# A two-block transformer forward: the opening projection by channel halves, and the modulation sums in another order

## The chip, the cores and the metric

One NeuronCore of a Trainium2 chip runs the whole program. The metric is the device time of one execution in microseconds (us); lower is better. Engines are named as the profile names them: PE is TensorE (PEld its weight loads), DVE is VectorE, ACT is ScalarE, POOL is GpSimd, SP is SyncE, which here only issues DMA transfers.

## What is computed

The reference is two blocks over 256 tokens of 1024 channels, all in float32. Only the head of block one matters for the change; in the reference it reads

```python
for l in range(DEPTH):
    mod = c @ w_ada[l] + b_ada[l]
    shift, scl, gate = jnp.split(mod, 3, axis=-1)
    h = rms_norm(x, g_norm[l]) * (1.0 + scl[:, None, :]) + shift[:, None, :]
    proj = h @ w_in[l]
    u_pool, z_pool, q, k, v, z_attn, m_pool, m_attn = jnp.split(proj, splits, axis=-1)
```

`mod` is a matrix times a vector (1024 by 3072); `h` is the normalised input, scaled and shifted per channel; `proj` is a 256x1024 by 1024x5120 product. After it come a pooling branch and an 8-head attention branch, two up-projections and an output projection. Block two has a modulation of its own (`w_ada_2`, 1024 by 6144), another input projection, retention and sparse attention, and a last layer that reads every row of two 16384x1024 tables.

## The kernel before, in words

**Panels.** Every weight matrix is cut into panels of 128 partitions by 4096 floats (2.1 MB): all 1024 input channels (8 groups of 128) for 512 output columns. The list `STREAM` names the panels in the order in which they are loaded, with their user: `"pe"` for a product on PE, `"dve"` for a modulation sum, `"row"` for a modulation panel that PE multiplies itself. Four slots in SBUF hold them; panel n goes into slot n mod 4. SP issues two transfers for each panel, one for each half (four channel groups), after it has waited until panel n-4 is used up (`panel_used`). `ada1` are the panels of `w_ada` (0, 1 shift, 2, 3 scale, 4, 5 gate; the even one for channels 0 to 511), `in1` those of `w_in`, `ada2` those of `w_ada_2`, `out1` the output projection.

**Modulation sums.** For a `"dve"` panel DVE forms the sum of the eight channel groups, each times a column of `c` (`ada`, `sum_step`: one tensor_scalar and seven scalar_tensor_tensor of 128x512). The running sum lies in SBUF (`acc`) for the first three, in a PSUM bank for those of block one after them, and in SBUF again for the last ones. Then PE adds up the partitions with a product by ones (step `("ada", n)`, or `start_columns` in the opening), and DVE adds the bias and stores scale or shift (`ada_out`, `start_scale`). `next_acc` at the end of a `proj` step says how far ahead of its panel a sum is made: all those whose panel stands less than 3 places behind the projection's panel, except the last two of the list (`ada_steps[:-2]`).

**Products in three thirds.** A float32 product is made as three faster ones, of a high part and a low part of each operand. ACT copies a half panel to its high part (`unit_high`, L814, step `("high", k)`), POOL subtracts to get the low part (`unit_low`, L740, four instructions for each half panel), and `products` (L1123, L1129, L1135) issues 24 matmuls of 128x512 for each half panel: high by high, low input by high weight, high input by low weight. `UNITS` lists the half panels in the order in which both are made. The input `h` itself is made from transposes (`xT`, L1068): ACT writes the modulated channels of token tile 1 and DVE those of tile 0 (L852, L1735), ACT makes their high part (L799), DVE the low part (L1807).

**Order.** `steps()` writes one list, and every engine walks it and does its own part of each step. Inside `heads`, the list mixes the eight attention heads (`score`, `pT`, `pv`) with the projections that follow. PSUM banks 0 to 3 are handed out in turn to the steps that need one, and a step waits until the use before it is freed.

**The opening.** SP loads ada1 2, 3, 0, 1 and then in1 2 and 3. DVE sums panels 2, 3 and 1; PE multiplies panel 0 as a row (`make_row`), ACT copies the row, and PE turns it into columns (`row_columns`). After all four, `mod_ready` goes up once, and ACT and DVE write `h` for all eight channel groups; then PE starts the product of in1 2. The rest of the modulation alternates with the panels of `in1` (ada1 4, in1 4, ada1 5, in1 5, ...).

## Time and profile before

| | us |
|---|---|
| runs, median of 3 | 1271.54 |
| lowest and highest run | 1267.73, 1272.63 |
| profiled execution, its own time | 1268.93 |
| its span in the trace | 1267.1 |
| PE busy in the span | 1193.6 |
| DVE, ACT, POOL busy | 904.5, 619.4, 551.6 |

The page gives one profiled execution: busy time of each engine, the span in 40 slices, the groups of instructions that cost most, and for the idle time before a group what ended it. A timeline row has start, duration, engine, line, operation, what is written from what, the count that was merged into the row, and in brackets the idle time before it with its releaser. A granted clock of 1.00 is 2.4 GHz on PE, 0.50 is 1.2 GHz. Times in the trace count from the start of the span.

### The profile page before, as it was taken

To read this page: it belongs to the slowest core of one execution; us is meant where nothing else is said; L and a number is where in the kernel's file an instruction comes from. 1 tells how busy PE (TensorE), PEld (TensorE's weight loads), DVE (VectorE), ACT (ScalarE), POOL (GpSimd) and SP (SyncE) were. 2 spreads that over 40 slices of the span, in tenths; PEclk is the share of its full clock that TensorE was granted. 3 is DMA by queue.
4 is the path that set the end of the run, shared out by engine and by line. 5 is a ranking of instruction groups with operands and counts; after the bars stand their busy time and mean duration, and the time that the engine had idled before them with its cause. 6 is when DMAs were issued, how large, how long until landed. Compare 5 with 4: busy or idle time off the path is not lost.

```text
span 1267.1 us, 19098 instructions
## 1 busy us (share of the span) xinstructions
PE 1193.6 (94%) x7186; PEld 1050.7 (83%) x7186; DVE 904.5 (71%) x1847; ACT 619.4 (49%) x1077; POOL 551.6 (44%) x323
## 2 busy tenths in 40 slices
PE   4899998899968899999999999999999999999996
PEld 2778876686747699999999999999888888888885
DVE  5678657676685643999948999999566656656566
ACT  2454444444533434444456666555445545444543
POOL 0968759474531202888877777766300000000000
PEclk9899999999978999999999999999999999999998
DMA  9988664354231431565544545455566666666664
GB/s 374 417 329 323 265 266 169 133 206 154 113 150 67 199 133 49 182 184 182 185 160 160 161 156 165 152 153 152 164 231 206 209 231 218 197 185 196 190 196 149
DMA packets 54523, 244.28 MB, mean 193 GB/s; under 512 B 6944, under 2 KB 7328, under 8 KB 42016
## 3 DMA queue, kind: packets, MB, share of 16 engines
q1 hardware_dynamic: 54000, 242.34, 55.4%
q8 instruction: 58, 0.95, 0.3%
q10 hardware_dynamic: 432, 0.72, 0.2%
q14 instruction: 33, 0.27, 0.1%
HBM read 240.94 MB, written 2.10 MB: 192 GB/s over the span
## 4 chain that ended last, share of the span: by engine, by line
PE 75%; DVE 4%; issue 1%; ACT 1%; POOL 0%; POOLq 0%; DVEq 0%; ACTq 0%
PE bank L1526 10%; PE bank L1523 10%; PE bank L1522 10%; PE banks L1562 5%; PE bank L1565 5%; PE bank L1568 5%; PE banks L1565 5%; PE bank L1562 5%; PE banks L1568 5%; PE banks L1536 3%; PE banks L1123 1%; PE banks L1129 1%; PE banks L1135 1%; PE banks L1393 1%; PE banks L1481 1%
## 5 line engine op out<-in xcount | busy, mean ns | idle before, releaser
L765 POOL TENSOR_TENSOR split_r<-ring,split_r 128x1024 fp32r<-128x1024 f32 x128 | 308.0, 2407 | 158.0 <-ACT split_r L996 157.9
L996 ACT ACTIVATE split_r<-ring 128x1024 fp32r<-128x1024 f32 x256 | 269.1, 1052 | 180.2 <-PE bank L1526 180.2
L1522 PE MATMUL bank<-h_high_r,split_r 128*128 128x256 f32 x1024 | 251.3, 283 | 1.7 <-ACT split_r L996 1.7
L1523 PE MATMUL bank<-h_low_r,split_r 128*128 128x256 f32 x1024 | 251.2, 283 | 0.0
L2147 DVE TENSOR_TENSOR split_r<-ring,split_r 128x1024 fp32r<-128x1024 f32 x128 | 156.8, 1225 | 65.6 <-ACT split_r L996 65.6
L1522 PEld LDWEIGHTS bank<-h_high_r,split_r 128*128 128x128 f32 x1024 | 196.3, 192 | 1.9 <-issue 1.9
L1523 PEld LDWEIGHTS bank<-h_low_r,split_r 128*128 128x128 f32 x1024 | 196.4, 192 | 0.0
L740 POOL TENSOR_TENSOR wq_low_r<-G,G_r 128x512 fp32r<-128x512 f32 (+1 forms) x104 | 135.2, 1336 | 68.5 <-ACT G_r L814 68.5
L769 POOL TENSOR_TENSOR small<-small 128x1 f32<-128x1 f32 x2 | 1.5, 760 | 359.0 <-DVE small L2173 359.0
L1526 PE MATMUL bank<-h_high_r,split_r 128*128 128x256 f32 x1024 | 143.7, 283 | 0.2 <-POOL split_r L765 0.2
L1050 ACT ACTIVATE gs_r<-G 128x256 fp32r<-128x256 f32 x128 | 53.5, 418 | 172.5 <-PE bank L1568 172.5
L1526 PEld LDWEIGHTS bank<-h_high_r,split_r 128*128 128x128 f32 x1024 | 132.1, 192 | 0.4 <-POOL split_r L765 0.4
L2095 DVE SCALAR_TENSOR_TENSOR hot_r<-bank,x,w_both_r 128x256 fp32r<-128x256 f32 x256 | 105.5, 473 | 0.0
L2145 DVE TENSOR_TENSOR gs_r<-G,gs_r 128x256 fp32r<-128x256 f32 x128 | 54.3, 424 | 61.8 <-ACT gs_r L1050 61.4
L740 POOL TENSOR_TENSOR wq_low_r<-G,hT_r 128x512 fp32r<-128x512 f32 x48 | 65.3, 1394 | 66.0 <-ACT hT_r L814 66.0
L1562 PE MATMUL banks<-split_r,gs_r 128*128 128x512 f32 x254 | 79.1, 393 | 1.8 <-ACT split_r L996 1.8
L1565 PE MATMUL bank<-split_r,gs_r 128*128 128x512 f32 x254 | 78.2, 389 | 0.0
L1562 PE MATMUL bank<-split_r,gs_r 128*128 128x512 f32 x254 | 78.2, 389 | 0.0
L1568 PE MATMUL banks<-split_r,gs_r 128*128 128x512 f32 x254 | 78.2, 389 | 0.0
L1568 PE MATMUL bank<-split_r,gs_r 128*128 128x512 f32 x254 | 78.2, 389 | 0.0
L1565 PE MATMUL banks<-split_r,gs_r 128*128 128x512 f32 x254 | 78.2, 389 | 0.0
L814 ACT ACTIVATE G_r<-G 128x2048 fp32r<-128x2048 f32 (+1 forms) x26 | 48.7, 1881 | 21.9 <-DMA G<-in_in 18.8
(453 smaller groups left out, 2242.1 us busy)
## 6 DMA issues: line engine op xcount, KB each, us to landing
ring<-in_down SPq DMA_DIRECT2D x128, 512.0 KB, 3.5
ring<-in_up SPq DMA_DIRECT2D x128, 512.0 KB, 3.5
G<-in_ada SPq DMA_DIRECT2D x32, 1024.0 KB, 10.5
G<-in_in SPq DMA_DIRECT2D x32, 1024.0 KB, 7.0
G<-in_out SPq DMA_DIRECT2D x8, 1024.0 KB, 8.1
G<-in_wq SPq DMA_DIRECT2D x8, 1024.0 KB, 7.7
tab<-in_ada SPq DMA_DIRECT2D x4, 1024.0 KB, 5.8
G<-in_poolup SPq DMA_DIRECT2D x2, 1024.0 KB, 6.1
```

Source lines behind the costliest of these rows:

```text
L740: pool.tensor_tensor(low[:, c, :], raw_half[:, c, :], high[:, c, :].bitcast(F32), ALU.subtract)\
L765: pool.tensor_tensor(wsplit[:, j % SPLIT, 1, :], raw[:, j % RAW, :], wsplit[:, j % SPLIT, 0, :].bitcast(F32), ALU.subtract).then_inc(low_r ...
L996: nc.scalar.activation(wsplit[:, n % SPLIT, 0, :], raw[:, n % RAW, :], ACT.Copy).then_inc(high_ready, 1)
L1522: mm(o, w[0][:, c, :], h_high[:, c, :], start=(c == 0), stop=False)
L1523: mm(o, w[0][:, c, :], h_low[:, c, :], start=False, stop=False)
L1526: ins = mm(o, w[1][:, c, :], h_high[:, c, :], start=False, stop=(c == C - 1))
L1562: mm(o, g[0][:, tok], w[:, 0, cols], start=(n == 0), stop=False, skip_group_check=True)
L1565: mm(o, g[1][:, tok], w[:, 0, cols], start=False, stop=False, skip_group_check=True)
L1568: ins = mm(o, g[0][:, tok], w[:, 1, cols], start=False, stop=False, skip_group_check=True)
L2095: ins = stt(out=O2[m % 2][:, t, :, :], in0=iota_p.unsqueeze(1).to_broadcast([P, 2, P]), scalar=picks[:, 1, tok:tok + 1], in1=w_both[:, :, ...
L2145: tt(gs[n % 2][1], Gv[:, n, :], gs[n % 2][0].bitcast(F32), ALU.subtract).then_inc(gs_low, 1)
L2147: tt(wsplit[:, n % SPLIT, 1, :], raw[:, n % RAW, :], wsplit[:, n % SPLIT, 0, :].bitcast(F32), ALU.subtract)\
```

## The change

**Order of the loads.** `STREAM` now begins ada1 2, 0, 3, in1 2, in1 3, ada1 1, and afterwards each pair has the `in1` panel first and the modulation panel second. The loads are issued from a list `LOADS`: the first halves of in1 2 and in1 3 are loaded ahead of ada1 1, their second halves behind it. Three rows of gate constants (1.5 MB) are loaded behind in1 5 and no longer behind in1 2, with a semaphore of their own.

**Opening by halves.** DVE sums ada1 2 and ada1 0, which are scale and shift of channels 0 to 511, and `mod_ready` goes up for these alone. `h` is made for them, and PE multiplies the first half of in1 2. PE makes the row from ada1 3 in two parts, with `start_columns(1)` between them. The step `mods` sums ada1 1 on DVE with the running sum in PSUM bank 7, and PE's `row_columns` and `start_columns(2)` stand between the first half of in1 2 and that of in1 3. The second halves of both follow. ACT makes the high parts of three half panels (`("high", 1)` to `("high", 3)`) ahead of the second part of `h`.

**Sums in the rest of block one.** The sum for a projection is now that of the panel just behind it, and `ada_steps[:-4]` leaves the last four to be placed by hand. The sum of ada2 6 (panel 22) is written into the list as single steps: four behind `upT` and four behind the first half of `poolup`, in SBUF. Its product by ones, and that of ada2 9, stand behind the last head.

PE in the opening: the names are `keep,tab` for columns from a sum (4 matmuls), `keep,G` 128x128 for the transposes, `G,small` for the row, `keep,G` 128x1 for its columns; then the thirds of a half panel, 8 matmuls each. Before:

```order
L1099 MATMUL banks<-keep,tab 128x1 x4
L1068 MATMUL bank<-keep,G 128x128 x8
L1068 MATMUL banks<-keep,G 128x128 x8
L1099 MATMUL banks<-keep,tab 128x1 x4
L1085 MATMUL bank<-G,small 1x512 x8
L1092 MATMUL bank<-keep,G 128x1 x4
L1099 MATMUL bank<-keep,tab 128x1 x4
L1123 MATMUL bank<-hT_0_r,ring_r 128x512 x8
L1129 MATMUL bank<-hT_0_r,G_r 128x512 x8
L1135 MATMUL bank<-wq_low_r,ring_r 128x512 x8
```

and with the change:

```order
L1105 MATMUL banks<-keep,tab 128x1 x4
L1075 MATMUL bank<-keep,G 128x128 x8
L1075 MATMUL banks<-keep,G 128x128 x8
L1090 MATMUL bank<-G,small 1x512 x4
L1105 MATMUL banks<-keep,tab 128x1 x4
L1090 MATMUL bank<-G,small 1x512 x4
L1129 MATMUL banks<-hT_0_r,ring_r 128x512 x8
L1135 MATMUL banks<-hT_0_r,G_r 128x512 x8
L1141 MATMUL banks<-wq_low_r,ring_r 128x512 x8
L1098 MATMUL bank<-keep,G 128x1 x4
L1105 MATMUL bank<-keep,tab 128x1 x4
L1129 MATMUL bank<-G_r,ring_r 128x512 x8
```

The row's columns and the third set of columns have moved behind the first half panel's 24 matmuls; the next half panel stands behind them.

DVE behind the last head: `tab<-G,small` is a sum (`tab<-G,small,tab` its steps in SBUF), `G_r<-...,ring_r` the low part of the pooled rows, `G<-G,bank` the evacuation of a half of `poolup`, `G<-bank,G` the step `y`. Before:

```order
L1978 TENSOR_TENSOR G_r<-banks,ring_r 128x4x128 x2
L1934 SCALAR_TENSOR_TENSOR G<-G,bank 128x512
L1934 SCALAR_TENSOR_TENSOR G<-G,banks 128x512
L1918 TENSOR_TENSOR G<-bank,G 128x512 x2
L1663 TENSOR_SCALAR tab<-G,small 128x512
L1665 SCALAR_TENSOR_TENSOR tab<-G,small,tab 128x512 x3
L1692 TENSOR_TENSOR small<-bank,small 128x4
```

and with the change:

```order
L2007 TENSOR_TENSOR G_r<-banks,ring_r 128x4x128
L2007 TENSOR_TENSOR G_r<-bank,ring_r 128x4x128
L1682 TENSOR_SCALAR tab<-G,small 128x512
L1684 SCALAR_TENSOR_TENSOR tab<-G,small,tab 128x512 x3
L1963 SCALAR_TENSOR_TENSOR G<-G,banks 128x512 x2
L1684 SCALAR_TENSOR_TENSOR tab<-G,small,tab 128x512 x4
L1947 TENSOR_TENSOR G<-bank,G 128x512 x2
L1682 TENSOR_SCALAR tab<-G,small 128x512
L1684 SCALAR_TENSOR_TENSOR tab<-G,small,tab 128x512 x3
L1716 TENSOR_TENSOR small<-bank,small 128x4
L1719 TENSOR_SCALAR small<-small 128x4
L1720 TENSOR_TENSOR small<-small 128x4
```

Eight sum steps have come in, four on either side of the evacuations, ahead of `y`; so has one more set of columns (three small instructions).

The diff, cut to what the prediction speaks of:

```diff
 STREAM = []
-STREAM += [("ada1", 2, PANEL, "dve"), ("ada1", 3, PANEL, "dve"), ("ada1", 0, PANEL, "row"), ("ada1", 1, PANEL, "dve")]
-STREAM += [("in1", 2, PANEL, "pe"), ("in1", 3, PANEL, "pe")]
-for a, b in ((("ada1", 4), ("in1", 4)), (("ada1", 5), ("in1", 5)), (("ada2", 2), ("in1", 0)), (("ada2", 3), ("in1", 1)),
-             (("ada2", 0), ("in1", 6)), (("ada2", 1), ("in1", 7)), (("ada2", 8), ("in1", 8)), (("ada2", 9), ("in1", 9))):
-    STREAM += [(*a, PANEL, "dve"), (*b, PANEL, "pe")]
+STREAM += [("ada1", 2, PANEL, "dve"), ("ada1", 0, PANEL, "dve"), ("ada1", 3, PANEL, "row"), ("in1", 2, PANEL, "pe"),
+           ("in1", 3, PANEL, "pe"), ("ada1", 1, PANEL, "dve")]
+for a, b in ((("in1", 4), ("ada1", 4)), (("in1", 5), ("ada1", 5)), (("in1", 0), ("ada2", 2)), (("in1", 1), ("ada2", 3)),
+             (("in1", 6), ("ada2", 0)), (("in1", 7), ("ada2", 1)), (("in1", 8), ("ada2", 8)), (("in1", 9), ("ada2", 9))):
+    STREAM += [(*a, PANEL, "pe"), (*b, PANEL, "dve")]
...
 START = 3
+LOADS = [(0, 0), (0, 1), (1, 0), (1, 1), (2, 0), (2, 1), (3, 0), (4, 0), (5, 0), (5, 1), (3, 1), (4, 1)]
+LOADS += [(n, half) for n in range(6, len(STREAM)) for half in range(2)]
...
 UNITS = [(AT[p], half) for p in SPLIT_PANELS for half in range(2)]
+UNITS[1:3] = UNITS[2:0:-1]
...
-    ada_after(AT[("in1", 2)], ada)
-    high("in1", 2, (0,))
-    out.extend(("xT", 0, t, half) for t in range(NT) for half in range(2))
-    high("in1", 2, (1,))
-    panel("in1", 2)
+    ada_after(AT[("in1", 4)], ada)
+    out.extend([("high", 0), ("xT", 0, 0, 0), ("xT", 0, 1, 0), ("xsplit", 0), ("row",), ("high", 1), ("high", 2), ("high", 3),
+                ("mods",), ("xT", 0, 0, 1), ("xT", 0, 1, 1), ("xsplit", 1), ("proj", "in1", 2, 0), ("proj", "in1", 2, 1)])
     panel("in1", 3)
     panel("in1", 4)
...
-    later += [[("upT", 0), ("upT", 1), ("high", 21)],
-              [("high", 22), ("up", "poolup", 0, 0), ("up", "poolup", 1, 0)]]
+    six = AT["ada2", 6]
+    later += [[("upT", 0), ("upT", 1), ("high", 21)] + [("sum", six, c) for c in range(4)],
+              [("high", 22), ("up", "poolup", 0, 0), ("up", "poolup", 1, 0)] + [("sum", six, c) for c in range(4, C)]]
     heads(0, H, later)
...
+            bank = 4 + s[2]
         else:
             bank = turn % 4
...
-            for n, (name, i, cols, user) in enumerate(STREAM):
-                if n >= SLOTS:
+            for n, half in LOADS:
+                name, i, cols, _ = STREAM[n]
+                if n >= SLOTS and half == 0:
...
-                if n == SLOTS:
+                if (n, half) == (4, 1):
                     sp.dma_start(tab[:, 0:n_tab], d["tab"]).then_inc(tables_in, 16)
-                    sp.dma_start(gateA, d["gate1"].partition_broadcast(P)).then_inc(tables_in, 16)
-                    sp.dma_start(gateB, d["gate3"].partition_broadcast(P)).then_inc(tables_in, 16)
-                    sp.dma_start(gfin, d["gfin1"].partition_broadcast(P)).then_inc(tables_in, 16)
-                if n == 2 * SLOTS:
+                if (n, half) == (2 * SLOTS, 1):
+                    sp.dma_start(gateA, d["gate1"].partition_broadcast(P)).then_inc(gates_in, 16)
+                    sp.dma_start(gateB, d["gate3"].partition_broadcast(P)).then_inc(gates_in, 16)
+                    sp.dma_start(gfin, d["gfin1"].partition_broadcast(P)).then_inc(gates_in, 16)
+                if (n, half) == (2 * SLOTS + 2, 1):
                     sp.dma_start(band, d["band"]).then_inc(band_in, 16)
                     sp.dma_start(wgrp, d["wgrp"]).then_inc(band_in, 16)
...
-            act.wait_ge(row_full, 1)
-            nc.scalar.activation(row, ps[6][0:1, :], ACT.Copy).then_inc(row_copied, 1)
...
+                elif kind == "row":
+                    act.wait_ge(row_full, 1)
+                    nc.scalar.activation(row, ps[6][0:1, :], ACT.Copy).then_inc(row_copied, 1)
+                elif kind == "xsplit":
+                    for q in range(NT):
+                        x0_high_part(q, s[1])
...
-                    if half == 0:
-                        act.wait_ge(mod_ready, blk_n + 1)
+                    act.wait_ge(mod_ready, half + 1)
...
-                    for q in range(NT):
-                        x0_high_part(q, half)
...
+            def make_row(half):
+
+                w = wait_panel(pe_, ROWS[0], (half,)).rearrange("p (c n) -> p c n", c=C)
+                for c in range(4 * half, 4 * half + 4):
+                    ins = mm(ps[6][0:1, :], c1[:, c:c + 1], w[:, c, :], start=(c == 0), stop=(c == C - 1))
+                if half == 1:
+                    ins.then_inc(row_full, 1)
...
-                    ins = mm(ps[4 + k][:, c:c + 1], acc[k % 2][:, c * P:(c + 1) * P], ones[:, 0:1], start=True, stop=True)
+                    ins = mm(ps[(2, 3, 6)[k]][:, 4 * (k == 2) + c:4 * (k == 2) + c + 1], acc[k % 2][:, c * P:(c + 1) * P], ones[:, 0:1], start=True, stop=True)
...
+            for half in range(2):
+                for t in range(NT):
                     pe_.wait_ge(xn_ready, t + 1)
-                transposes(("xT", 0, t, half), [xn[0][:, t, (4 * half + c) * P:(4 * half + c + 1) * P] for c in range(4)])
+                    transposes(("xT", 0, t, half), [xn[0][:, t, (4 * half + c) * P:(4 * half + c + 1) * P] for c in range(4)])
+            make_row(0)
             start_columns(1)
-            make_row()
-            row_columns()
-            start_columns(2)
+            make_row(1)
+
...
+            def in1_products(i, halves, fill):
...
+            in1_products(2, (0,), True)
+            row_columns()
+            start_columns(2)
+            in1_products(3, (0,), True)
+            in1_products(2, (1,), False)
+            in1_products(3, (1,), False)
...
-                part = ps[4 + k % 2][:, :] if START <= k < BLOCK_ONE else a
+                part = ps[7][:, :] if k == START - 1 else ps[4 + k % 2][:, :] if START <= k < BLOCK_ONE else a
...
-            def start_scale(k):
-
-                dve.wait_ge(start_cols, k + 1)
-                c4 = slice(4 * k, 4 * k + 4)
-                link(tt(modA[:, 0, c4], ps[4 + k][:, 0:4], b1c[:, 8 + 4 * k:12 + 4 * k], ALU.add))
+            def start_scale(half, src):
+
+                c4 = slice(4 * half, 4 * half + 4)
+                link(tt(modA[:, 0, c4], src[:, 0:4], b1c[:, 8 + 4 * half:12 + 4 * half], ALU.add))
                 link(ts(modA[:, 0, c4], modA[:, 0, c4], 1.0, None, ALU.add))
                 link(tt(modA[:, 0, c4], modA[:, 0, c4], gcol[:, 0, c4], ALU.mult))
+
+            def start_shift(half, src):
+
+                c4 = slice(4 * half, 4 * half + 4)
+                link(tt(modB[:, 0, c4], src[:, 0:4], b1c[:, c4], ALU.add))
+                dve.sem_inc(mod_ready, 1)
 
             dve.wait_ge(first_in, 16)
             next_acc()
             next_acc()
             dve.wait_ge(consts_in, 16 * 7)
-            for k in range(2):
-                start_scale(k)
-            next_acc()
-            dve.wait_ge(row_cols, 1)
-            tt(modB[:, 0, 0:4], ps[7][:, 0:4], b1c[:, 0:4], ALU.add)
-            dve.wait_ge(start_cols, 3)
-            link(tt(modB[:, 0, 4:8], ps[6][:, 0:4], b1c[:, 4:8], ALU.add))
-            dve.sem_inc(mod_ready, 1)
+            dve.wait_ge(start_cols, 1)
+            start_scale(0, ps[2])
+            dve.wait_ge(start_cols, 2)
+            start_shift(0, ps[3])
...
-                elif s == ("xT", 0, 1, 1):
...
+                elif kind == "mods":
+                    next_acc()
+                    dve.wait_ge(row_cols, 1)
+                    dve.wait_ge(start_cols, 3)
+                    start_scale(1, ps[6])
+                    start_shift(1, ps[6][:, 4:8])
+                elif kind == "xsplit":
+                    half = s[1]
+                    dve.wait_ge(x0_high_ready, 2 + 2 * half)
+                    for t in range(NT):
+                        evacuated(dve, ("xT", 0, t, half))
...
-                    ahead = [a for a in ada_steps[:-2] if a[1] < AT[(s[1], s[2])] + 3]
+                    ahead = [a for a in ada_steps[:-4] if a[1] < AT[(s[1], s[2])] + 3]
```

## Rows read from the trace of the kernel before

**Rows 1.** Stretches of PE alone: us, busy, PE clock, DMA share, GB/s.

```profile
20.40:22.40 2.00, 0.89 (x8) 1.00 1.01 422
...
35.60:38.80 3.20, 3.10 (x7) 0.50 1.05 416
...
43.60:49.10 5.50, 5.50 (x25) 1.00 1.01 422
...
72.00:188.00 116.00, 113.25 (x582) 1.00 0.73 292
```

**Rows 2.** Timeline of DVE in the opening: start, us, instruction, idle before.

```profile
15.46 0.49 DVE L1663 TENSOR_SCALAR tab<-G,small 128x512 f32<-128x512 f32 x1 [2.49 <-DMA G<-in_ada]
15.98 5.48 DVE L1665 SCALAR_TENSOR_TENSOR tab<-G,small,tab 128x512 f32<-128x512 f32 x7
...
25.51 0.48 DVE L1663 TENSOR_SCALAR tab<-G,small 128x512 f32<-128x512 f32 x1 [2.27 <-DMA G<-in_ada]
...
35.54 1.62 DVE L1807 TENSOR_TENSOR G_r<-G,ring_r 128x1024 fp32r<-128x1024 f32 x1
```

**Rows 3.** Timeline of PE in the opening.

```profile
22.49 7.03 PE L1085 MATMUL bank<-G,small 128*1 128x512 f32 x16
...
31.56 1.05 PE L1099 MATMUL bank<-keep,tab 128*128 128x1 f32 x8 [0.31 <-DVE tab L1665]
...
35.70 3.75 PE L1123 MATMUL bank<-hT_r,ring_r 128*128 128x512 f32 x8 [3.09 <-DVE G L1735]
...
60.85 2.08 PE L1123 MATMUL bank<-G_r,ring_r 128*128 128x512 f32 x8 [0.48 <-issue]
```

**Rows 4.** Timeline of ACT in the opening.

```profile
30.37 1.91 ACT L814 ACTIVATE hT_r<-G 128x2048 fp32r<-128x2048 f32 x1
...
32.97 1.50 ACT L852 ACTIVATE G<-banks,small 128x128 f32<-128x128 f32 x4 [0.68 <-DVEq L1777]
34.36 1.15 ACT L799 ACTIVATE ring_r<-G 128x512 fp32r<-128x512 f32 x2
```

**Rows 5.** Timeline of POOL, opening and last heads.

```profile
32.36 5.95 POOL L740 TENSOR_TENSOR wq_low_r<-G,hT_r 128x512 fp32r<-128x512 f32 x4 [17.10 <-ACT hT_r L814]
...
185.99 5.23 POOL L740 TENSOR_TENSOR wq_low_r<-G,G_r 128x512 fp32r<-128x512 f32 x4
191.19 6.34 POOL L740 TENSOR_TENSOR wq_low_r<-G,ring_r 128x512 fp32r<-128x512 f32 x4
198.64 6.92 POOL L740 TENSOR_TENSOR wq_low_r<-G,hT_r 128x512 fp32r<-128x512 f32 x4 [1.11 <-ACT hT_r L814]
```

**Rows 6.** Line 1665 until 215 us: ns min/median/max, first and last start.

```profile
L1665 DVE SCALAR_TENSOR_TENSOR banks<-G,small,banks x54: 754/756/757, 52.5 to 168.7; 128x512 f32<-128x512 f32 x54
L1665 DVE SCALAR_TENSOR_TENSOR tab<-G,small,tab x28: 739/752/1670, 7.5 to 201.0; 128x512 f32<-128x512 f32 x28
```

**Rows 7.** Timeline of DVE behind the last head.

```profile
184.45 0.69 DVE L1934 SCALAR_TENSOR_TENSOR G<-G,bank 128x512 f32<-128x512 f32 x1 [4.33 <-PE bank L1135]
185.36 0.69 DVE L1934 SCALAR_TENSOR_TENSOR G<-G,banks 128x512 f32<-128x512 f32 x1 [0.22 <-PE banks L1135]
187.22 1.29 DVE L1918 TENSOR_TENSOR G<-bank,G 128x512 f32<-128x512 f32 x2 [1.17 <-PE bank L1310]
188.72 1.35 DVE L1663 TENSOR_SCALAR tab<-G,small 128x512 f32<-128x512 f32 x1 [0.22 <-DVE G L1918]
190.11 5.04 DVE L1665 SCALAR_TENSOR_TENSOR tab<-G,small,tab 128x512 f32<-128x512 f32 x3
195.18 0.16 DVE L1692 TENSOR_TENSOR small<-bank,small 128x4 f32<-128x4 f32 x1
```

**Rows 8.** Timeline of PE behind the last head.

```profile
186.95 1.00 PE L1197 MATMUL bank<-keep,tab 128*128 128x1 f32 x8
...
195.49 0.63 PE L1068 MATMUL bank<-keep,G 128*128 128x128 f32 x4 [1.51 <-DVE small L1692]
```

**Rows 9.** Timeline of ACT: the first high part of poolup.

```profile
166.86 1.92 ACT L814 ACTIVATE ring_r<-G 128x2048 fp32r<-128x2048 f32 x1 [2.47 <-DMA G<-in_poolup]
```

More of the change, by code:

```diff
@@ L246 @@
             bank = 4 + s[3]
+        elif s[0:2] == ("xT", 0) and s[3] == 1:
+            bank = 4 + s[2]
         else:
@@ L835, in _ @@
                     if (t, half) == (0, 0):
-                        act.wait_ge(mod_ready, b + 1)
+                        act.wait_ge(mod_ready, b + 2)
                     dst, ready = (x1_high, x1_high_ready) if b == 1 else (h_high, h_high_ready)
@@ L1091, in row_columns @@
                 for c in range(4):
-                    ins = mm(ps[7][:, c:c + 1], row[:, c * P:(c + 1) * P], ones[0:1, 0:1], start=True, stop=True)
+                    ins = mm(ps[6][:, c:c + 1], row[:, c * P:(c + 1) * P], ones[0:1, 0:1], start=True, stop=True)
                 ins.then_inc(row_cols, 1)
@@ L1206, in _ @@
                     if t == 0:
[L1207 to L1214 removed]
+                        in1_products(i, (0, 1), True)
                 elif kind in ("unit", "third"):
@@ L1683, in ada_out @@
                     g = gateA if name == "ada1" else gate2
+                    if name == "ada1" and half == 0:
+                        dve.wait_ge(gates_in, 48)
                     if name == "ada2" and half == 0:
```

54 lines of the change are left out of this document (22 added, 32 removed).

## Prediction

> **What bounds the kernel now.** I read the stretches of the trace first, then the timelines of all engines in the opening and behind the last head. From 72 to 188 us PE is busy 113.25 of 116 us at full clock [rows 1]: time won before 72 us is carried on, and time lost behind 188 us is not given back by it. Only two places are left in which the change can act: the opening, where PE waits for the modulation, and the place behind the last head, to which the sum of ada2 6 has been moved.
>
> In the opening the loads are the bound. The core takes 420 GB/s [rows 1], which is 2.5 us for each half panel (1.05 MB); the first half of ada1 3 has landed when DVE starts on it at 15.46, that of ada1 1 four half panels later, at 25.51 [rows 2]. PE starts its first product only at 35.70, after a wait of 3.09 us [rows 3]: the modulation of all channels comes ahead of it (ada1 1 landed, summed by 31.5, columns at 31.56). That product runs at a granted clock of 0.50, half of 2.4 GHz [rows 1], so that 8 matmuls take 3.75 us; at 43.6 the clock is 1.00 and 25 matmuls take 5.50. A half panel of 24 matmuls is thus 5.45 us, including its weight waits. In1 4 starts at 60.85 [rows 3].
>
> **The opening, step by step.** The loads in the new order land, at 2.5 us each from the anchor 15.5: ada1 0 at 15.5 and 18.0, ada1 3 at 20.5 and 23.0, the first halves of in1 2 and in1 3 at 25.5 and 28.0, ada1 1 at 30.5 and 33.1, the second halves at 35.6 and 38.1, the tables at 41.2, in1 4 at 43.7 and 46.2.
> - DVE ends its second sum at 21.5 as before (15.98 plus 5.48 [rows 2]). PE's first row half takes half of 7.03 us [rows 3], from 20.5 to 24.0, and the columns 1.05: shift and scale of the first channels are there at 25.4. That costs nothing, because ACT makes the high part of in1 2 first: 25.5 to 27.5 [rows 4].
> - ACT then writes `h` (1.50) and its high parts (1.15) [rows 4]: 30.2. PE's first product starts there, 5.5 us earlier than 35.70. DVE's low part takes 1.6 [rows 2]; POOL's low weights, 5.95 from 27.5 [rows 5], come at 33.5 and are needed at 33.9. The half panel ends at 35.7.
> - DVE's sum of ada1 1 starts at 31.8, behind that low part. In PSUM a step is 0.76 us as in SBUF [rows 6], 6.2 us for eight: 38.0. PE waits for it from 36.2, and with it the first half of in1 3, which is queued behind; columns until 39.1. That half ends at 44.6.
> - Columns to scale and shift (0.7, with POOL busy perhaps 2.5), `h` and high parts (2.7) end at 44.5 at the latest, so the second halves follow without a wait: in1 2 ends at 50.0, in1 3 at 55.5. POOL's four units of 5.0 to 5.2 us end at 48.7 and are no bound. Their high parts lie in ACT's waits; were they late, POOL's last unit (needed at 53.6) would have 5 us to spare.
> - In1 4 (landed at 46.2) starts at 55.6 instead of 60.85: **5.2 us won**. This needs full clock. The idle stretches are 1.7 us (28.5 to 30.2) and 2.0; 1.1 us idle at 20.4 to 22.4 left the clock at 1.00, 3.09 us brought it to 0.50 [rows 1, 3]. The new ones lie between. One stretch of 3 us at half clock costs 1.5; I take off half of that, 0.8. **Term: -4.4**, bounds -5.2 and -2 (the full loss as in [rows 3], 3.2 us).
>
> Costed at nothing: the later modulation panels. Each is now issued behind its in1 panel and summed one projection later, but the sum (6.3 us) still fits in a projection of 11; one set of columns (1.00 us on PE [rows 8]) only moves to the end. The gate constants now load behind in1 5, 15 us before its use. A second cost hides there: ada2 6 stands ahead of poolup in SP's queue and waits for in1 8, so poolup, whose high part starts at 166.86 upon its landing [rows 9], lands 5 us later. ACT's evacuations of in1 9 stand behind it, 1.7 us late at most, against a set of columns that has gone (-0.9): I take +0.
>
> **Behind the last head.** I count in the times of before; the shift of the opening comes on top. The sum of ada2 6 used to be made during in1 9, with its partial in PSUM. Now its eight steps are in SBUF: four behind the low part of the pooled rows, where DVE was idle for 4.33 us, and four behind the evacuation that ends at 186.05 [rows 7]. POOL works there without a pause until 197.5 [rows 5]. A step in SBUF beside a busy POOL is 1.67 us (three in 5.04 [rows 7]; the longest of 28 is 1.670, of the 54 in PSUM 0.757 [rows 6]). So the first four fit roughly; the second four end at 186.05 + 6.7 = 192.8.
> - PE wants this sum's columns behind those of ada2 9, at 187.9 (186.95 plus the one more set [rows 8]), and the second half of poolup is queued behind: PE stands for 4.9 us.
> - On DVE `y`, at 187.22 before [rows 7], starts at 192.8; the four steps of ada2 7 behind it (1.35 and 5.04) and the new set of columns (0.5) put the one that frees PE's bank from 195.18 to about 201. PE waited for just this (1.51 us at 195.49 [rows 8]), then ACT turns out the heads and makes the high part with which POOL starts at 198.64 [rows 5]; POOL is then busy for 30 us. So the delay is passed on.
> - Delay 5.9, less some tenths because POOL may be through before DVE's last steps. **Term: +5.5.** Lower bound: steps at the 0.78 us spacing of the opening (5.48 for seven [rows 2]), 3.1 us for four, delay 1.9. Upper bound: 8, if the first four run over as well.
>
> Nearest to the truth is the row at 190.11: the same operation, with POOL in the same work, 4 us further on. The Trainium skill, SBUF — State Buffer, section Who interferes with whom, is harsher: a DVE instruction with two SBUF inputs and a POOL instruction that reads SBUF lock each other out for whole instructions. By that rule a step behind one of POOL's 1.25 us instructions would be 2.0 us, four would be 8.1, and the term would be +7 to +8; the longest step in the trace, 1.67, is less than that.
>
> **Sum.** -4.4 + 5.5 = +1.1. The profiled execution had 1268.93 us, so its successor would have 1270.0; the median of the runs, 1271.54, lies 2.6 above it, and with +1.1 becomes **1272.6 us**. A difference of under 0.5% (6.4 us) is about what a measurement of this kernel can't tell from none, so I forecast no change.
>
> **Rivals.**
> - *The sum stops PE and the stop costs the clock* (slower). PE idle for 5 us at 188 to 193 is longer than the 3.09 that brought 0.50 in the opening, and the second half of poolup would then run at half rate (16 matmuls at 0.43 instead of 0.23, +3.2) while POOL is late too: delay 9.5. It decides if the opening also loses its 3.2: -2 + 9.5 = +7.5, **1279.0**. Against it: DVE's chain covers PE's half rate in part. Chance 0.15.
> - *The sums find gaps and the opening runs at full clock* (faster). Delay 1.9; the opening wins the 5.5 of its start and all of the lost 3.2, if the sum of ada1 1 is early enough for PE not to stand: -8.7 + 1.9 = -6.8, **1264.7**. For it: 4 of the 8 steps lie in a stretch where DVE was idle. Against it: POOL is busy from 181 to 197.5, and the sum of ada1 1 can't start before 31.8. Chance 0.12.
> - *The change does not do what it says*: the first product starts early, but PE soon waits for ada1 1 and for the low weights, and in1 4 starts where it did. 0 + 5.5 = +5.5, **1277.0**, still within 0.5%. Chance 0.12.
>
> The forecast itself has 0.61. Faster by over 0.5% is 0.12, slower 0.15, and 0.61 + 0.12 = 0.73 within it. The range runs from the forecast's bounds, -5.2 + 1.9 = -3.3 and -2 + 8 = +6, with 1.5 to 2.5 us for the spread of the runs on either side: 1265.5 to 1279.0. It leaves out the second rival and half of the first, about 0.2.
>
> **What would show it.** Right: first product at about 30, in1 4 at 55 to 57; DVE's SBUF steps of ada2 6 at 1.67 us beside POOL; a wait of PE of some 5 us for `acc` ahead of the second half of poolup; POOL's unit behind 198.64 only 0 to 2 us from where it was. Wrong: no such wait, or steps of 0.75 there (then the loss is mis-sized and the kernel is faster by 3 or more); or a start of in1 4 at 59 or later (then the opening's gain is).

## The result, and the profile after

| | before | after |
|---|---|---|
| median of 20 runs, us | 1269.65 | 1273.26 |
| lowest, highest | 1266.64, 1272.82 | 1270.68, 1286.21 |
| profiled execution: own time, span | 1268.93, 1267.1 | 1271.72, 1269.9 |
| mean granted clock | 0.980 | 0.975 |
| PE, DVE, ACT, POOL busy | 1193.6, 904.5, 619.4, 551.6 | 1199.7, 916.3, 619.4, 554.7 |

The ratio is 1.0039, with a 95% interval of 1.0025 to 1.0053. The quotient of the two medians is 1.0028, and their difference +3.6 us; the forecast was +1.1 and no change by more than 0.5%. The interval lies above 1, so the change is a little slower. Four of the change's 20 runs lie at 1278 to 1286 us; the highest of before is 1272.82. Where ratios and medians disagree below, both are given.

First the opening. Timeline of PE after:

```profile
29.52 2.08 PE L1129 MATMUL banks<-hT_r,ring_r 128*128 128x512 f32 x8 [1.02 <-ACT ring_r L803]
...
36.89 1.05 PE L1105 MATMUL bank<-keep,tab 128*128 128x1 f32 x8 [0.68 <-DVE tab L1684]
37.80 3.67 PE L1129 MATMUL bank<-G_r,ring_r 128*128 128x512 f32 x8
...
57.09 2.08 PE L1129 MATMUL banks<-G_r,ring_r 128*128 128x512 f32 x8 [1.10 <-issue]
```

The first product starts at 29.52 and no longer at 35.70 [rows 3]. PE waits 0.68 us for the sum of ada1 1, then 8 matmuls take 3.67 us (2.08 at 29.52), which is the half clock again. In1 4 starts at 57.09 in place of 60.85: 3.8 us won. Its wait of 1.10 us ("issue") is explained by DVE, which frees the bank only now:

```profile
53.93 1.35 DVE L1661 TENSOR_TENSOR G<-G,ring 128x64 f32<-128x64 f32 x1
55.20 1.32 DVE L1662 TENSOR_TENSOR G<-G,ring 128x64 f32<-128x64 f32 x1
56.44 0.55 DVE L1846 COPY G<-banks 128x384 f32<-128x384 f32 x1
```

The copy ends at 56.99 and PE starts 0.1 us later. The two instructions ahead of it, on 128x64, take 1.35 and 1.32 us beside POOL; in the opening alone (below), where POOL had nothing to do at that point, the same two took 0.23 and 0.22. With one set of columns moved away, the lead at the first head is 4.57 us (75.57 before, 71.00 after), and PE carries it to the last heads.

Then the last head. PE after:

```profile
174.72 0.90 PE L1308 MATMUL bank<-keep,ring 128*128 128x128 f32 x3 [2.64 <-DVE ring L1745]
...
176.55 3.76 PE L1129 MATMUL banks<-ring_r 128*128 128x512 f32 x8
...
191.01 1.84 PE L1223 MATMUL banks<-keep,tab 128*128 128x1 f32 x8 [3.92 <-DVE tab L1684]
192.71 2.05 PE L1129 MATMUL banks<-hT_r,ring_r 128*128 128x512 f32 x4
...
202.75 1.17 PE L1129 MATMUL banks<-G_r,ring_r 128*128 128x512 f32 x4 [0.83 <-ACT ring_r L937]
```

and the same two places of PE before:

```profile
177.83 0.55 PE L1289 MATMUL bank<-keep,ring 128*128 128x128 f32 x3 [1.18 <-DVE ring L1724]
...
179.62 1.16 PE L1123 MATMUL bank<-ring_r 128*128 128x512 f32 x4 [0.63 <-DVE G_r L1978]
...
187.81 1.17 PE L1123 MATMUL bank<-hT_r,ring_r 128*128 128x512 f32 x4
...
196.90 1.16 PE L1123 MATMUL bank<-G_r,ring_r 128*128 128x512 f32 x4 [0.78 <-ACT ring_r L930]
```

DVE and POOL after, over the same stretch:

```profile
169.43 0.90 DVE L1719 TENSOR_SCALAR small<-small 128x4 f32<-128x4 f32 x1
170.37 1.18 DVE L1720 TENSOR_TENSOR small<-small 128x4 f32<-128x4 f32 x1
...
172.82 1.18 DVE L1734 TENSOR_SCALAR small<-small 128x2 f32<-128x2 f32 x1
...
177.44 4.14 DVE L1684 SCALAR_TENSOR_TENSOR tab<-G,small,tab 128x512 f32<-128x512 f32 x3
...
185.10 5.77 DVE L1684 SCALAR_TENSOR_TENSOR tab<-G,small,tab 128x512 f32<-128x512 f32 x4
```

```profile
169.04 4.95 POOL L746 TENSOR_TENSOR wq_low_r<-G,ring_r 128x512 fp32r<-128x512 f32 x4 [12.61 <-ACT ring_r L818]
...
177.87 6.09 POOL L746 TENSOR_TENSOR wq_low_r<-G,hT_r 128x512 fp32r<-128x512 f32 x4 [3.89 <-ACT hT_r L818]
...
204.49 6.74 POOL L746 TENSOR_TENSOR wq_low_r<-G,hT_r 128x512 fp32r<-128x512 f32 x4 [8.16 <-ACT hT_r L818]
```

Two of the small instructions of DVE before:

```profile
174.21 0.16 DVE L1699 TENSOR_TENSOR small<-small 128x4 f32<-128x4 f32 x1
...
176.96 0.17 DVE L1713 TENSOR_SCALAR small<-small 128x2 f32<-128x2 f32 x1
```

Windows of PE after, at the two stretches behind its waits (us, busy, granted clock, DMA share, GB/s):

```profile
176.00:180.00 4.00, 4.00 (x12) 0.50 0.99 420
...
192.00:196.00 4.00, 4.00 (x12) 0.50 0.93 346
```

Read together they give a ledger of after minus before, at the start of the same work of PE:

| place | before | after | difference | step |
|---|---|---|---|---|
| first head | 75.57 | 71.00 | -4.57 | |
| last head's transposes | 177.83 | 174.72 | -3.11 | +1.46 |
| evacuation of poolup's first half ends (DVE) | 186.05 | 185.18 | -0.87 | +2.24 |
| second half of poolup | 187.81 | 192.71 | +4.90 | +5.77 |
| attnup | 196.90 | 202.75 | +5.85 | +0.95 |
| low third behind POOL's unit | 242.62 | 248.29 | +5.67 | -0.18 |
| transposes of block two | 276.78 | 280.54 | +3.76 | -1.91 |
| end | 1267.1 | 1269.9 | +2.8 | -0.96 |

The four plus steps are these. (1) Poolup lands when it did (its high part is made at 167.05, before at 166.86) though all else is 4.6 us earlier, so POOL's unit for it, 169.04 to 173.99, lies over DVE's small instructions of the last head: three take 0.90 to 1.18 us, each of which took 0.16 or 0.17 us before. (2) Behind the wait of 2.64 us the clock is 0.50. (3) PE stands for 3.92 us in front of the sum of ada2 6, and its columns, the additional set, take 1.84 us at half clock and not 1.00: 5.76 of the 5.77. (4) The second half of poolup starts at half clock too. When PE comes to the transposes behind it, at 200.89, it doesn't wait: DVE had freed their banks by 198.46. So in the change it is PE's own row that brings the delay to attnup.

### The profile page after: what moved, and what is told of

Same layout as the page of the kernel before. It is cut to its first block, busy times and chain, and to the rows that moved or that the text cites. A ratio compares the mean times of both kernels' runs of the same rounds, so it can differ in the third digit from the quotient of the medians.

```text
span 1269.9 us, 19103 instructions
## 1 busy us (share of the span) xinstructions
PE 1199.7 (94%) x7186; PEld 1054.6 (83%) x7186; DVE 916.3 (72%) x1847; ACT 619.4 (49%) x1077; POOL 554.7 (44%) x323
## 4 chain that ended last, share of the span: by engine, by line
PE 74%; DVE 4%; issue 1%; ACT 1%; POOL 0%; POOLq 0%; DVEq 0%; ACTq 0%
PE bank L1545 10%; PE bank L1542 10%; PE bank L1541 10%; PE banks L1581 5%; PE bank L1581 5%; PE banks L1587 5%; PE bank L1584 5%; PE bank L1587 5%; PE banks L1584 5%; PE banks L1555 3%; PE banks L1129 1%; PE banks L1135 1%; PE banks L1141 1%; PE bank L1412 1%; PE banks L1160 1%; PE banks L1169 1%
```

## The experiments

Each kernel was timed in 8 to 12 runs beside runs of before on the same chip; the second time is the median of these. Kernels that start from the change have "change" over their diff.

**The change again.** No edit.

> The change once more, as it is, for a second profile and for a ratio on the chip of the next runs. Theory A (what the change loses it loses in three places, each time in the same way): 3 to 4 us above before, with PE idle for 2.6 us near 172 us, idle for 3.9 us near 187 us, and both stretches behind them at a granted clock of 0.50. Theory B (the clock falls by chance): the same time on average, but the granted clock stays at 1.00 behind one of the two waits.

1273.11 us against 1269.69 before, ratio 1.0028 (1.0016 to 1.0040). In its profile PE waits 2.71 us at 174.51 and 4.00 us at 190.72, and the granted clock is 0.50 in 176 to 180 and in 188 to 196. Theory A: the two falls come back.

**Poolup loaded first.** Change:

```diff
-STREAM += [("ada2", 6, PANEL, "dve"), ("poolup", None, PANEL, "pe"), ("attnup", None, PANEL, "pe"), ("ada2", 7, PANEL, "dve"),
+STREAM += [("poolup", None, PANEL, "pe"), ("ada2", 6, PANEL, "dve"), ("attnup", None, PANEL, "pe"), ("ada2", 7, PANEL, "dve"),
...
-    for n in ada_after(AT[("poolup", None)], ada):
+    for n in ada_after(AT[("attnup", None)], ada):
```

> Poolup is loaded ahead of ada2 6; all else as in the change. Theory A (poolup lands late, so that POOL's unit for it, 169.0 to 174.0, lies over DVE's small instructions of the last head, three of which take 0.9 to 1.2 us in place of 0.17; PE then waits 2.6 us and loses its clock): the unit starts near 164, the small instructions take 0.17 us, PE waits 1.2 us at the last head, the granted clock is 1.00 behind it, and the end comes 3 to 4 us earlier, about the time of before. Theory B (DVE's sums behind the last head set the time, whatever comes ahead of them): no gain, the time of the change within 1 us. Theory C (ada2 6, now landing 5 us later, is late for its sum at 177): the wait of PE at 187 grows by up to 4 us, and nothing is won.

1273.71 against 1269.69, ratio 1.0030 (1.0015 to 1.0046): nothing won. PE:

```profile
173.12 0.55 PE L1308 MATMUL bank<-keep,ring 128*128 128x128 f32 x3 [1.18 <-DVE ring L1745]
...
174.91 3.54 PE L1129 MATMUL banks<-ring_r 128*128 128x512 f32 x8 [0.64 <-DVE G_r L2007]
```

The step from load to small instructions is right: POOL's unit is at 164.26, the scalar instruction takes 0.17 us, the wait is 1.18 us. Three things work against the gain. The clock fell all the same (3.54 us for 8 matmuls); the wait for ada2 6 was 4.49 us, where that of the change repeated was 4.00; and out1 0, whose slot is now that of poolup, landed only at 204.04, so that POOL's unit for it started at 206.04, 2.0 us later than in the change repeated. How much each took is not separated, and the profiled execution (1275.66) lies 2.0 us above the median. A panel's place in the list also decides which later panel waits for it; no theory had that.

**Ada2 6 in PSUM.** Change:

```diff
-                    sum_step(n, k, c, acc[k % 2], acc[k % 2])
+                    sum_step(n, k, c, ps[4 + k % 2][:, :] if STREAM[n][0:2] == ("ada2", 6) else acc[k % 2], acc[k % 2])
```

> The eight steps of ada2 6 stay where the change puts them, but their running sum lies in a PSUM bank. Theory A (the steps take 1.4 us each because DVE and POOL both work in SBUF): seven of the steps take 0.76 us, the second four end 2.7 us earlier, PE waits 1.2 us and not 3.9 for them, the granted clock stays at 1.00 in the second half of poolup, and the end comes 3 to 5 us earlier than with the change. Theory B (the steps are slow whatever they read, POOL stretches all of DVE's work): steps of 1.4 us again, and the time of the change. Theory C (POOL's unit for the output projection is held by another thing than DVE): steps of 0.76, but under 1 us won.

1269.22 against 1269.69, ratio 1.0016 (0.9994 to 1.0037). That is 3.9 us below the change on the same chip by the medians, but 1.5 by the ratios, whose intervals overlap; two of the twelve runs lie at 1279. So the gain in time is likely and not shown; what the edit does to the steps is. DVE and, below, POOL:

```profile
184.28 2.33 DVE L1684 SCALAR_TENSOR_TENSOR banks<-G,small,banks 128x512 f32<-128x512 f32 x3
186.65 0.75 DVE L1684 SCALAR_TENSOR_TENSOR tab<-G,small,banks 128x512 f32<-128x512 f32 x1
...
177.36 5.04 POOL L746 TENSOR_TENSOR wq_low_r<-G,hT_r 128x512 fp32r<-128x512 f32 x4 [2.66 <-ACT hT_r L818]
182.34 4.99 POOL L746 TENSOR_TENSOR wq_low_r<-G,G_r 128x512 fp32r<-128x512 f32 x4
```

A step is 0.75 us beside a POOL that never stops, four take 3.1 us in place of 5.77, POOL's own unit is back from 6.09 to 5.04, and PE's wait is 1.27 us, as theory A had it. The clock did not hold: it was 0.73 in 188 to 192. The Trainium skill, SBUF — State Buffer, section Who interferes with whom, says that a DVE instruction with at most one SBUF input, outside the 2-port perf modes, doesn't contend with GpSimd; here the trace agrees for these steps, 0.75 us against 1.44. Two of the slow small instructions of the change (0.90 us at 169.43, 1.18 at 172.82) have one tensor as input, too; whether they run in such a mode, no run here shows.

**Ada2 6 early.** Change, with the eight steps also taken out of the list:

```diff
-                    ahead = [a for a in ada_steps[:-4] if a[1] < AT[(s[1], s[2])] + 3]
+                    ahead = [a for a in ada_steps[:-3] if a[1] < AT[(s[1], s[2])] + 3]
```

> The sum of ada2 6 is made during in1 9 again, behind that of ada2 9, with its running sum in PSUM; its columns stay behind the last head. The opening is that of the change. Theory A (the opening is a gain of 3.8 us, and all of the loss lies behind the last head): 4 to 6 us earlier than the change, 1 to 2 below before; what is left of the loss is poolup's late landing. Theory B (DVE can't make two sums of 6.3 us in one projection of 11 beside the heads): the second sum pushes DVE's work on the last heads 3 to 6 us back, PE waits there, and the time is that of the change or above.

1271.46 against 1269.69, ratio 1.0017 (1.0005 to 1.0030): 1.7 us below the change by the medians, 1.4 by the ratios, whose intervals overlap; not 4 to 6. The second sum starts at 169.27 only, after 3.60 us of waiting for PE's columns of ada2 8, whose buffer it takes; it ends at 175.56, and PE, which needs a bank behind it, is idle for 4.10 us at 175.77. Theory B. So the sum of ada2 6 can't simply go back: with each sum one projection later, in1 9 would have to hold two.

**PSUM and poolup first together.** Change, with both edits above and

```diff
-           ("out1", 0, PANEL, "pe"), ("out1", 1, PANEL, "pe")]
+           ("out1", 1, PANEL, "pe"), ("out1", 0, PANEL, "pe")]
-LOADS += [(n, half) for n in range(6, len(STREAM)) for half in range(2)]
+LOADS += [(n, half) for n in [*range(6, 26), 27, 26, *range(28, len(STREAM))] for half in range(2)]
-BLOCK_ONE = sum(n < AT["out1", 0] for n in ADA)
+BLOCK_ONE = sum(n < AT["out1", 1] for n in ADA)
```

> The change with both: ada2 6's running sum in PSUM, and poolup loaded ahead of ada2 6; the second half of the output projection's weights (out1 1) takes poolup's slot and is loaded behind the first (out1 0), so that POOL's unit for out1 0 does not wait for a load as it did when poolup alone was moved. Theory A (the two losses are separate and add): PE waits 1.2 us at the last head and about 1.3 us behind it, POOL's unit for out1 0 starts at 197 to 198 us, and the time is 1 to 2 us below that of the kernel with the sum in PSUM alone, 2 to 3 below before. Theory B (the clock falls behind either wait, whatever its length): the waits shorten as said, but the granted clock is 0.50 behind them all the same, and under 1 us is won.

1267.25 against 1269.34, ratio 0.9994 (0.9972 to 1.0017). PE:

```profile
172.32 0.55 PE L1308 MATMUL bank<-keep,ring 128*128 128x128 f32 x3 [1.18 <-DVE ring L1745]
174.12 2.09 PE L1129 MATMUL banks<-ring_r 128*128 128x512 f32 x8 [0.63 <-DVE G_r L2007]
...
183.75 1.84 PE L1223 MATMUL banks<-keep,tab 128*128 128x1 f32 x8 [1.27 <-DVE tab L1684]
...
195.25 1.17 PE L1129 MATMUL banks<-G_r,ring_r 128*128 128x512 f32 x4 [0.83 <-ACT ring_r L937]
```

The waits are as forecast and full clock holds behind the first, not behind the second. Attnup starts 7.1 us earlier than in the change repeated (202.31), of which the span keeps 6.3 (1263.0 against 1269.3); 0.7 of the 7.1 was there at the first head, since this execution kept full clock in the opening. The profiled execution is 2.4 us below the median of its kernel. The median is 2.1 below before, but three of the twelve runs lie at 1273.6 to 1276.9, and the interval holds 1.

**The relocation alone.** The kernel before with the eight steps in the list and `ada_steps[:-4]`; opening and load order as before.

> The kernel before, with one part of the change: the sum of ada2 6 in eight steps behind the last head, in SBUF. The opening, the load order and all else are as before (ada2 6 and then poolup are loaded as before, so that poolup does not move). Theory A (this relocation alone is the loss): POOL's unit behind the last heads starts 5 to 7 us later than 198.6, steps of 1.4 us, PE waits 4 us near 191, and the time is 5 to 7 us above before. Theory B (it only hurts together with the earlier opening, where poolup comes late): under 3 us above before.

1275.67 against 1269.34, ratio 1.0050 (1.0033 to 1.0068): +6.3. PE waits 5.31 us at 193.56, DVE's second four take 6.31 us. Attnup starts at 205.01 in place of 196.90, from a last head that stood 0.48 earlier: a delay of 8.6, of which 1.6 comes from a fall of the clock in the first half of poolup. Theory A: the loss needs nothing of the new opening.

**The opening alone.** Change, with the old order behind it:

```diff
-    STREAM += [(*a, PANEL, "pe"), (*b, PANEL, "dve")]
+    STREAM += [(*b, PANEL, "dve"), (*a, PANEL, "pe")]
...
-    ada_after(AT[("in1", 4)], ada)
+    ada_after(AT[("ada1", 4)], ada)
...
-    six = AT["ada2", 6]
-    later += [[("upT", 0), ("upT", 1), ("high", 21)] + [("sum", six, c) for c in range(4)],
-              [("high", 22), ("up", "poolup", 0, 0), ("up", "poolup", 1, 0)] + [("sum", six, c) for c in range(4, C)]]
+    later += [[("upT", 0), ("upT", 1), ("high", 21)],
+              [("high", 22), ("up", "poolup", 0, 0), ("up", "poolup", 1, 0)]]
...
-                    ahead = [a for a in ada_steps[:-4] if a[1] < AT[(s[1], s[2])] + 3]
+                    ahead = [a for a in ada_steps[:-2] if a[1] < AT[(s[1], s[2])] + 3]
```

> The opening of the change (ada1 2, 0, 3, in1 2 and 3, ada1 1 by halves), then the order of before: each modulation panel ahead of its in1 panel, the sum of ada2 6 during in1 9 in PSUM. Theory A (the opening is worth 3.8 us and keeps it to the end): in1 4 starts at 57 to 58 us, PE waits at the last head and behind it as before (1.2 and 1.5 us), and the time is 3 to 4 us below before. Theory B (what the opening wins is lost again at the last heads, since poolup's load or a fall of the clock does not move with it): within 1 us of before.

1273.63 against 1269.34, ratio 1.0035 (1.0021 to 1.0049); neither theory. Both expectations took the loads behind the opening as given, but in1 4 now takes the slot of in1 2, which is used up late:

```profile
61.82 2.48 PE L1128 MATMUL banks<-G_r,ring_r 128*128 128x512 f32 x8 [1.85 <-ACT G_r L817]
...
80.13 1.72 PE L1074 MATMUL banks<-keep,G 128*128 128x128 f32 x8 [4.25 <-ACT G L884]
```

ACT waits for loads there (in1 4's first half until 59.66, in1 5's until 75.11). The gate constants (1.5 MB) may play a part, too: they follow panel 8, which here is ada1 5 and not in1 5, and so stand ahead of in1 5 in SP's queue. What each of the two costs was not tested. As far as this kernel goes, the new opening needs the other half of the change, each sum one panel later, and with it the eight steps get their late place.

This profile is that of the slowest of the twelve runs (1279.94, 6.3 us above the median), and it shows one thing that the ten other profiles with this opening don't:

```profile
43.35 5.58 DVE L1834 TENSOR_TENSOR G_r<-G,ring_r 128x1024 fp32r<-128x1024 f32 x1 [1.22 <-ACT ring_r L802]
...
42.87 4.97 POOL L745 TENSOR_TENSOR wq_low_r<-G,hT_r 128x512 fp32r<-128x512 f32 x4
...
48.98 3.24 PE L1134 MATMUL banks<-G_r 128*128 128x512 f32 x8 [3.46 <-DVE G_r L1834]
```

DVE's low part of `h` takes 5.58 us and POOL's unit beside it 4.97. In the ten others it is 1.86 to 1.89 for DVE and 6.01 to 6.05 for POOL. PE stands for 3.46 us, the clock is 0.71 in 48 to 52, and the product ends some 5 us later than with full clock (59.97 against 54.6 in the kernel with the wait filled). This would account for most of the 6.3 us. It is a candidate for the high single runs of the other kernels with this opening; none of those was profiled.

**The wait filled.** Change; sixteen matmuls on PE whose result nobody uses, ahead of the wait for ada2 6:

```diff
+                    name, i = STREAM[n][0], STREAM[n][1]
+                    if (name, i) == ("ada2", 6):
+                        f = UNIT[AT["poolup", None], 1]
+                        pe_.wait_ge(split_high, f + 1)
+                        for j in range(16):
+                            mm(ps[5][:, :], up_high[0][:, j % 4, 0:P], unit_views(f)[1][:, j % 4, :], start=True, stop=True)
                     pe_.wait_ge(acc_ready, k + 1)
-                    name, i = STREAM[n][0], STREAM[n][1]
```

> The change, but PE does sixteen matmuls that nobody uses (3.6 us at full clock, into a bank that is free) while it waits for the sum of ada2 6 near 187 us. The wait stays. Theory A (the wait costs its own length and, behind it, about 2.5 us of half clock): PE is idle for under 1 us there, the granted clock stays at 1.00 in the second half of poolup, the heads are turned 1.5 to 2.5 us earlier and the time is that much below the change. Theory B (DVE and POOL are late anyhow, so PE's clock there costs nothing): full clock, and under 0.7 us won.

1271.15 against 1269.34, ratio 1.0012 (1.0001 to 1.0023). Windows of PE:

```profile
184.00:188.00 4.00, 4.00 (x26) 1.00 0.00 0
188.00:192.00 4.00, 3.87 (x22) 1.00 0.30 76
192.00:196.00 4.00, 4.00 (x20) 1.00 0.99 420
```

The sum comes when it did, the clock stays at 1.00, attnup starts at 198.88, and the median is 1.8 us above its own before, where that of the change repeated was 3.4 above: 1.6 us won, 2.0 by the ratios (their intervals overlap). The trace gives the same size at the place itself: from the first products of poolup to attnup 23.56 us, in the change repeated 25.97, 2.4 less. That is the price of the half clock there, apart from the wait: theory A. PE, now ahead, waits for DVE's chain (0.50 us at 196.87).

**Columns later.** The kernel with PSUM and poolup first, with the step of ada2 6's columns behind the second half of poolup.

> The kernel with ada2 6's sum in PSUM and poolup ahead, and PE now makes the columns of ada2 6 behind the second half of poolup and not ahead of it, so that it need not wait for the sum. Theory A (even the short wait of 1.3 us behind the last head costs the clock, as it did in both kernels with the sum in PSUM): no wait near 184 us, granted clock 1.00 through the second half of poolup, the heads turned 1 to 2 us earlier, the time 1 to 2 us lower. Theory B (DVE's next sum, three steps in 4.1 us beside POOL, holds the turning of the heads at 192 to 193 us, whatever PE does): full clock, but PE waits for DVE behind poolup instead, and under 0.7 us is won.

1268.06 against 1268.70, ratio 1.0001 (0.9987 to 1.0014). Theory B: no wait at 184, but PE is idle for 2.34 us at 192.99, until DVE is through four steps of ada2 7, and the clock falls there. Attnup starts at 196.73, 22.6 us behind the transposes of the last head (174.12); in the kernel without this edit it was 22.9 (195.25 and 172.32). So the edit wins 0.3 us at this place.

**Before, with one high part first.** The kernel before:

```diff
+    out.append(("high", 24))
     out.extend(("oT", t) for t in range(NT))
     out.extend(("sum", last, c) for c in range(4, C))
-    out.extend([("high", 24), ("high", 25)])
+    out.append(("high", 25))
```

> The kernel before, with one step moved: ACT makes the high part of out1 0's first half ahead of its two evacuations of the turned heads, and not behind them. Theory A (from there on POOL's row of units is what PE waits for, so a delay of POOL's first unit is passed on whole, and so is a gain): POOL's unit starts 2.0 to 2.4 us earlier than 198.64, at 196.3 to 196.6, and the time is 1.5 to 2.4 us below before. Theory B (PE's own products set the time up to 228 us): POOL's unit starts earlier, the waits of PE for it at 222 and 242 us get shorter, but the end comes under 0.7 us earlier, or later, since the turned heads now come up to 1.4 us later.

1267.66 against 1268.70, ratio 0.9989 (0.9979 to 0.9999). Its execution runs 2.24 us behind from the opening on. Less that, POOL's unit starts at 197.44, 1.2 us earlier, since POOL itself is busy until then; PE's wait at 222 is gone, and the low third at 242 comes 0.84 us earlier. Between the theories: POOL's row passes a shift on, but not whole. The interval ends just below 1.

**All together.** The last two edits in one.

> All of it: the change, ada2 6's sum in PSUM, poolup ahead, the columns later, and the high part of out1 0 ahead of the turned heads. Theory A: POOL's unit for out1 0 starts at 193 to 195 us, 4 to 5 us earlier than before, and the time is 5 to 6 us below before. Theory B (the parts hide one another): within 1 us of the better of the kernels with fewer of them.

1269.38 against 1268.70, ratio 1.0009 (0.9996 to 1.0022). POOL's unit starts at 193.44, but its later ones wait 2.03 and 7.18 us for ACT, which in the second case itself waited for PE, and PE waits 2.14 and 2.36 us for DVE. Theory B, and worse: the median lies above before, where that of the kernel with PSUM and poolup first was 2.1 below its own. That the two edits hinder each other is how I read it; the clock also fell in the first half of poolup here (3.52 us for 8 matmuls), and not in that kernel.

**Best guess.** The kernel with PSUM and poolup first, eight unused matmuls in the wait, and the high part first.

> The kernel with ada2 6's sum in PSUM and poolup ahead, with its columns in their old place, plus eight matmuls that nobody uses (1.8 us) on PE while it waits for that sum, plus the high part of out1 0 ahead of the turned heads. Theory A (in that kernel the clock falls behind the wait of 1.3 us, and ACT's order holds POOL back by about 1 us): full clock in the second half of poolup, PE still in front of the sum until 0.5 us before it comes, POOL's unit for out1 0 at 195 to 196 us, and the time 1 to 2 us below that kernel, 3 to 4 below before. Theory B (what is won behind the last heads is given back within 60 us, as in the kernel with all together, because POOL's later units wait for PE's progress): under 0.7 us below that kernel.

1264.85 against 1267.76, ratio 0.9988 (0.9965 to 1.0011). POOL's unit starts at 194.12 and the clock is 1.00 through the second half of poolup, but attnup starts at 195.16, no earlier than in the kernel without the last two edits. The clock fell in the first half of poolup (3.61 us for 8 matmuls, 2.09 there), which put PE 1.6 us back, and ACT's evacuations are late (PE waits 1.52 us for them and not 0.83). Against its own before it is 2.9 us lower where that kernel was 2.1, 0.8 more: theory B, nearly. It has the lowest runs of all (1262.85), but the interval holds 1, again with three runs at 1273.6 to 1274.8. What sets these apart was not profiled and stays open; the candidate is the long DVE instruction of the opening alone. So no version with the new opening is shown to beat before. The only interval below 1 is that of before with one high part first, and it ends at 0.9999.

## Why the prediction held, and where its steps did not

**The opening** was right. First product: 30.2 forecast, 29.5 measured. PE's wait for ada1 1 came where it was put, but was 0.7 us and not 2.0. In1 4: forecast 55.6 at full clock and 0.8 more for the chance of a fall, measured 57.09 with one. In the four kernels with the change's start and its load order in which the clock stayed at 1.00 it started at 55.70 to 56.18, in the six with a fall at 56.82 to 57.27; the 1.1 us for the bank was missing from the sum. The rival in which the opening wins nothing is out. The lead of 4.57 us at the first head is close to the term of 4.4, but not for its reasons alone: 3.8 of it were won by in1 4, and the rest comes with the set of columns moved away, which the forecast had set off against poolup's landing.

**The sum's steps** were nearly right: 1.67 us each, 6.7 for four; measured 1.44 and 5.77, and the first four fitted into DVE's idle time, as said. So the rival in which the sums find gaps is out, too. The lock over whole instructions that the Trainium skill states (SBUF — State Buffer, section Who interferes with whom) would have given 2.0 and 8.1 by my reading; for these steps the measurement decides against that size, and for its rule on one SBUF input. The one DVE instruction of 5.58 us beside a POOL unit of undiminished 4.97 is nearer to such a lock. "PE stands for 4.9 us" was 3.92. The step that failed is the next one, **"Delay 5.9 ... Term: +5.5"**: the ledger has +10.4 from the first head to attnup. The wait of 3.92 us and the set of columns of 1.00, 4.9 together, are what the term was for. Three things were not in it.
- *Poolup 5 us later, "costed at nothing"*: +1.46. The cover that I named (ACT's evacuations) held; the cost came through POOL, whose unit moved onto DVE's small instructions. All five kernels with poolup first had the wait of 1.18 us back.
- *Half clock in the first half of poolup*: +2.24.
- *Half clock behind the stop*: 0.84 in the columns and 0.95 in the second half, 1.8; the filled wait gave 1.6 to 2.0 back. I had this as the slower rival, with 0.15. Its mechanism happened, at once and in each profile with the stop; its delay of 9.5 was close to the 10.4. It did not decide because it was tied there to an opening that loses its gain, and the opening kept it. Its counter-argument, DVE's chain covers PE's half rate in part, failed: the banks that the forecast saw as the carrier of the delay were free by 198.46, and PE came to them at 200.89 without a wait.

One of the signs that I had set for being right did not come either: POOL's unit behind 198.64 was to start 0 to 2 us from there, and it started at 204.49, 5.85 later.

That the time was nearly met nonetheless is in part luck, twice. First, the forecast of 1272.6 stands on a median of three runs, 1271.54; that of 20 is 1269.65. The base was 1.9 too high and the change (+3.6 against +1.1) 2.5 too low, so that 1273.26 came out close. Second, 2.9 us came back behind 248 us. Of these, some 1.9 are a second fall of the clock that before has and the change has not, at 259.55 behind a wait of 1.77 us (1.18 after); of the other kernels only the one with the wait filled shows it, 0.74 and 0.84 in 260 to 268. Before with one high part first, which is otherwise the same kernel, kept 1.00 there, so that before need not fall each time. The last 0.96 us I can't place. The relocation alone cost 6.3 us in the medians, near to the term of 5.5; the new opening's gain of 4.6 less that is +1.7, and poolup's late landing, which only the two together have, is the likely rest; that sum is an argument and no run.

Small slips in the working: the figures for DVE's chain add up to a delay of 6.1 and not 5.9, those of the first rival to 9.1 and not 9.5, and the lower end of the range to 1265.7 and not 1265.5. None of them decides anything.

## What to carry over

A sum whose running total lies in SBUF should not be moved beside a busy POOL; in a PSUM bank the same eight steps took 6.2 us in place of 10.4, and POOL got a sixth of its unit back. When everything but one load moves earlier, look at what that load starts (here ACT, then POOL) and which instructions of a third engine it now covers. A stop of PE like those of 2.6 to 5.3 us here should be priced with what half clock costs the work behind it, here 2 us on top of 4. Executions are best compared from a common point, such as the last head: in the kernels with the same opening in1 4 started anywhere between 55.70 and 57.27.

## What was not expected of the hardware

- Waits of the same length don't always bring the same clock. Behind waits of 1.18 and 0.63 us at the last head eight matmuls took 2.1 us in five profiles (before, two kernels of the change's family, the opening alone, the high part first) and the clock fell in four others (3.5 to 3.6 us in three of them). Behind each of the nine waits of 2.6 us or more at the last heads it fell. What makes the difference at 1.2 us is open.
- DVE's smallest instructions (128x4 and 128x2) go from 0.17 us to between 0.9 and 1.2 beside POOL, five to seven times as long, while a step of 128x512 only doubles. For a chain of small ones that is the larger price.
- The same DVE instruction (128x1024, both inputs in SBUF) beside the same unit of POOL took 1.86 to 1.89 us in ten profiles and 5.58 in one. In the ten POOL was slowed (6.0 us for its unit), in the one it was not (4.97). What decides between them is open.
